# A linear recurrence over eight heads: levels merged, decays in PSUM, head norms on four columns, heads finished inside, output projection begun early

## What is computed

```
f = lb + (1 - lb) * sigmoid(f_pre);  k = 1 - f;  q = silu(q_pre);  v = i_in
b = cumsum(log f) within a chunk of tokens
o_inter = (q * exp(b)) @ state
a[t, s] = sum_d q[t,d] k[s,d] exp(b[t,d] - b[s,d])      for s <= t
o_intra = a @ v
state = exp(b_last) * state + (k * exp(b_last - b))^T @ v
o = o * rsqrt(mean(o*o over the 128 value channels) + eps)
o = o * out_norm * silu(g_pre);  h = h + o @ w_out
```

## Time and profile before

| | |
|---|---|
| median of 3 runs | 3115.41 us (3114.5 to 3117.74) |
| the profiled execution | 3111.95 us, its span 3110.0 us |
| PE busy | 3021.6 us, 97% of the span |
| DVE busy | 2407.8 us, 77% |
| ACT busy | 1193.4 us, 38% |
| POOL busy | 1310.9 us, 42% |
| hg_i's last matmul begins | 1661.6 us |
| the levels run | 1677 to 1810 us |
| hg_out runs | 1822 to 1879 us |

### The profile page before, as it was taken

One profiled execution on the slowest core, in us unless ns is written; L12 is line 12 of the kernel. 1 busy time (PEld: TensorE's weight loads), 2 busy tenths in 40 slices (PEclk: granted clock), 3 DMA queues, 4 the chain that ended last, 5 costly groups with the idle time before them and its releaser, 6 DMA issues.

```text
span 3110.0 us, 44566 instructions
## 1 busy us (share of the span) xinstructions
PE 3021.6 (97%) x16468; PEld 2672.1 (86%) x16468; DVE 2407.8 (77%) x4496; ACT 1193.4 (38%) x1842; POOL 1310.9 (42%) x749
## 2 busy tenths in 40 slices
PE   7999999999999999999998979999999999999998
PEld 5657899999998888887787967899999998888887
DVE  5345899988877888888235876899888978888887
ACT  4433333444433333333333433333444433333333
POOL 3313465444434444443344423465444444444442
PEclk9999999999999999999998989999999999999999
DMA  3202367999999999998221002367999999999996
GB/s 136 73 21 96 99 201 253 341 375 356 374 365 376 372 355 351 356 348 293 88 95 48 1 28 95 102 201 265 336 379 357 373 368 389 361 349 362 351 357 254
DMA packets 345719, 800.86 MB, mean 258 GB/s; under 512 B 27936, under 2 KB 191776, under 8 KB 345248
## 3 DMA queue, kind: packets, MB, share of 16 engines
q1 hardware_dynamic: 271776, 529.55, 48.9%
q0 software_dynamic: 73728, 268.47, 22.7%
HBM read 695.15 MB, written 102.76 MB: 257 GB/s over the span
## 4 chain that ended last, share of the span: by engine, by line
PE 92%; DVE 3%; DMA 2%; ACT 1%; issue 1%; POOL 0%; SPq 0%; ACTq 0%; DVEq 0%
PE PS L1361 27%; PE PS L1363 27%; PE PS L1362 27%; PE PS L1529 3%; PE PS L1626 2%; PE PS L1601 2%; DMA arena<-acts_dram 1%; DVE arena L1327 1%; PE PS L1506 1%; PE PS L1484 1%; DMA acts_dram<-arena 1%; PE PS L1467 1%; PE PS L1466 0%; POOL w_lo L509 0%; DMA w_raw<-in_mla_t 0%
## 5 line engine op out<-in xcount | busy, mean ns | idle before, releaser
L1361 PE MATMUL PS<-x_hi,w_hi 128*128 128x384 f32 (+1 forms) x2616 | 924.9, 354 | 14.7 <-issue 7.5
L586 ACT ACTIVATE w_hi<-w_raw 128x1024 fp32r<-128x1024 f32 x609 | 643.0, 1057 | 699.5 <-PE PS L1363 685.4
L1363 PE MATMUL PS<-x_hi,w_lo 128*128 128x384 f32 (+1 forms) x2616 | 908.3, 347 | 0.0
L1362 PE MATMUL PS<-x_lo,w_hi 128*128 128x384 f32 (+1 forms) x2616 | 907.0, 347 | 0.0
L520 POOL DMA_INDIRECT arena<-in_v_t,arena x256 | 445.1, 1738 | 599.5 <-DVE resid L1173 551.0
L1361 PE MATMUL PS<-w_hi,x_hi 128*128 128x512 f32 x1744 | 682.1, 391 | 12.8 <-POOL w_lo L509 8.6
L1362 PE MATMUL PS<-w_lo,x_hi 128*128 128x512 f32 x1744 | 680.2, 390 | 0.0
L1363 PE MATMUL PS<-w_hi,x_lo 128*128 128x512 f32 x1744 | 679.9, 390 | 0.0
L509 POOL TENSOR_TENSOR w_lo<-w_raw,w_hi 128x1024 fp32r<-128x1024 f32 x169 | 417.7, 2476 | 616.1 <-ACT w_hi L586 616.1
L1150 DVE TENSOR_TENSOR w_lo<-w_raw,w_hi 128x1024 fp32r<-128x1024 f32 x440 | 537.2, 1221 | 107.2 <-ACT w_hi L586 106.9
L520 POOL DMA_INDIRECT arena<-in_u_rows,arena x256 | 380.5, 1486 | 487.7 <-DVE arena L1157 434.5
(11 more groups left out here) (178 smaller groups left out, 2483.7 us busy)
## 6 DMA issues: line engine op xcount, KB each, us to landing
w_raw<-in_u_t SPq DMA_DIRECT2D x256, 512.0 KB, 6.9
w_raw<-in_v_t SPq DMA_DIRECT2D x256, 512.0 KB, 6.7
acts_dram<-arena SPq DMA_DIRECT2D x256, 192.0 KB, 7.4
gates_dram<-arena SPq DMA_DIRECT2D x24, 2048.0 KB, 15.9
arena<-gates_dram SPq DMA_DIRECT2D x64, 768.0 KB, 7.4
arena<-acts_dram SPq DMA_DIRECT2D x256, 192.0 KB, 7.1
w_raw<-in_hg_t SPq DMA_DIRECT2D x40, 512.0 KB, 3.2
w_raw<-in_pq_t SPq DMA_DIRECT2D x32, 512.0 KB, 3.2
```

Source lines behind the costliest of these rows:

```text
L586: act.activation(w_hi[:, slot, :], w_raw[:, slot, :], ACT.Copy).then_inc(hi_ready, 1)
L1361: pe.matmul(ps, wh, xh, start=start, stop=False)
L1362: pe.matmul(ps, wh, xl, start=False, stop=False)
L1363: return pe.matmul(ps, wl, xh, start=False, stop=stop)
```

## The change

It does these things.

1. **Merged levels.** k and q now lie 4096 elements apart with k first, so one access pattern (`keys_and_queries`) names the first halves of k and the second halves of q, and a level is scaled by one DVE instruction of 512 columns. ACT writes the exponentials into PSUM banks 2 and 3 (`scaling`), no longer back into `diff`. So POOL may refill `diff` when ACT is done with it, and `a` has banks 0 and 1 alone.
2. **One matrix a for a head.** `mask_level` writes the diagonal level by a product with its mask and each further level with `copy_predicated` into the places of the same 128x512 matrix. The values are multiplied once for each head (4 matmuls), behind level 7.
3. **Head norms on four columns.** ACT squares; TensorE takes each chunk's squares as the stationary operand and one column of ones as the moving one, which leaves 128x4 sums with tokens on partitions. Mean, root and reciprocal are of 128x4 for a head, the root in three batches (heads 0-3, 4-6, 7). The reciprocal roots come back across partitions by `diagonal` (ACT, four 128x128 products of the identity with a column) and `spread` (TensorE, ones by diagonal).
4. **Heads 0 to 3 are finished (gated, hi, lo) inside heads 6 and 7's levels**, and the first half of their output projection (banks 0 to 3, "project") stands between the last heads' spreads. `hg_out`'s other half rows follow.
5. **hg_i ends token by token** (`APART` = 2 weight tiles at the end instead of 1), its copies out stand among the first levels on ACT, and the four weight tiles of hg_out that POOL and ACT prepared between hg_i and the levels are now prepared in heads 1 and 2.
6. **In all three norms between stages** ACT's last two `next_high` calls stand behind the squares and roots. Before, one of them did (in the norm ahead of the recurrence none).

```diff
+SPREAD_AT = {(5, 6): 0, (6, 3): 1, (6, 6): 2, (7, 3): 3}
+ROOTS = [(0, 4), (4, 7), (7, 8)]
...
-        if n >= 2:
-            yield ("values", *divmod(n - 2, 8))
-            if (n - 2) % 8 == 7:
-                yield "ho", (n - 2) // 8, 0
+            if (h, p) in SPREAD_AT:
+                yield "spread", SPREAD_AT[h, p], 0
+        if n >= 2 and (n - 2) % 8 == 7:
+            yield "values", (n - 2) // 8, 0
+            yield "ho", (n - 2) // 8, 0
...
+    yield "spread", 4, 0
+    yield "project", 0, 0
     yield "hss", HEADS - 1, 0
+    yield "spread", 5, 0
+    yield "spread", 6, 0
+    yield "project", 2, 0
+    yield "spread", 7, 0
...
+        def keys_and_queries(h, m):
+            both = arena[:, h * SEQ:h * SEQ + SEQ]
+            return bass.AP(both.tensor, both.offset,
+                           [list(both.ap[0]), [2 * m, SEQ // (2 * m)], [HEADS * SEQ + m, 2], [1, m]])
...
 # POOL
-                    if (n - 2) % 8 == 0:
-                        pool.wait_ge(sem("k_decayed"), (n - 2) // 8 + 1)
-                    else:
-                        pool.wait_ge(sem("level_x"), (n - 2) // 8 * LEVELS + (n - 2) % 8)
+                    pool.wait_ge(sem("level_exp"), n - 1)
...
-            lows(BASE["hg_q"], BASE["hg_out"] + RING - 1)
+            lows(BASE["hg_q"], BASE["hg_i"] + 8)
             pool.wait_ge(sem("cumulated"), HEADS)
-            for n in range(2):
+            for n in range(8 * HEADS):
                 take_diff(n)
-            lows(BASE["hg_out"] + RING - 1, BASE["hg_out"] + RING)
-            for n in range(2, 8 * HEADS):
-                take_diff(n)
+                if n in range(11, 11 + 2 * RING, 2):
+                    lows(BASE["hg_out"] + (n - 11) // 2, BASE["hg_out"] + (n - 11) // 2 + 1)
...
 # ACT, norm between stages, and the stage ahead of it
-                elif last_tile is not None:
-                    next_high(last_tile)
+                else:
+                    for n in range(last_tile - APART + 1, last_tile + 1):
+                        next_high(n)
-            for n in range(7):
+            for n in range(8 - APART):
                 next_high(BASE["mla_out"] + n)
...
+            def level_exp(n):
+                h, k = divmod(n, 8)
+                act.wait_ge(sem("level_diff"), n + 1)
+                scaling_used(act, n - 2)
+                ...
+                act.activation(halves(scaling(n))[:, :, 0], halves(d)[:, :, 0], ACT.Exp, scale=-1.0)
+                act.activation(halves(scaling(n))[:, :, 1], halves(d)[:, :, 1], ACT.Exp)\
+                   .then_inc(sem("level_exp"), 1)
+            def head_out(h):
+                ready(act, ("ho", h))
+                act.activation(gk[:, h, :], PSb(("ho", h)), ACT.Square).then_inc(sem("head_sq"), 1)
+                free(act.activation(gq[:, h, :], PSb(("ho", h)), ACT.Copy), ("ho", h))
...
+                    if (h, k) == (5, 2):
+                        roots(0)
+                    if (h, k) in ((5, 4), (6, 1), (6, 4), (7, 1)):
+                        diagonal({(5, 4): 0, (6, 1): 1, (6, 4): 2, (7, 1): 3}[h, k], 0)
+                    if (h, k) in ((6, 1), (6, 6), (7, 1), (7, 6)):
+                        gated_high({(6, 1): 0, (6, 6): 1, (7, 1): 2, (7, 6): 3}[h, k])
...
 # DVE
-                for half, src in enumerate((gk, gq)):
-                    ins = dve.tensor_tensor(halves(xx[:, x % 2, :])[:, :, half],
-                                            halves(src[:, h, :])[:, :, half], halves(d)[:, :, half], ALU.mult)
-                ins.then_inc(sem("level_x"), 1)
+                dve.tensor_tensor(halves(xx[:, x % 2, :]), keys_and_queries(h, P >> k), halves(d), ALU.mult)\
+                   .then_inc(sem("level_x"), 1)
...
+                free(dve.copy_predicated(kept, where, given), ("a", h, p))
...
+                if (h, k) in ((6, 0), (6, 5), (7, 0), (7, 5)):
+                    gated({(6, 0): 0, (6, 5): 1, (7, 0): 2, (7, 5): 3}[h, k])
+                if (h, k) in ((6, 2), (6, 7), (7, 2), (7, 7)):
+                    gated_low({(6, 2): 0, (6, 7): 1, (7, 2): 2, (7, 7): 3}[h, k])
...
 # PE
-            token_major("hg_i", 8, 0, lambda kc: None)
-            was_freed(pe, ("hg_i", 7))
+            token_major("hg_i", 8, 0, lambda kc: None, APART)
...
-                    end(pe.matmul(PSb(("hss", h)), ones, gk[:, h, :], start=True, stop=True), ("hss", h))
+                    for c in range(TT):
+                        mm = pe.matmul(PSb(("hss", h))[:, c:c + 1], gk[:, h, c * P:(c + 1) * P], ones[:, 0:1],
+                                       start=True, stop=True)
+                    end(mm, ("hss", h))
```

More of the change, by code:

```diff
@@ L123, in __init__ @@
         self.signals = 0
-        self.count = {"act": 0, "dve": 0, "exp": 0, "state": 0, "kd": 0, "sum": 0}
+        self.count = {"act": 0, "dve": 0, "exp": 0, "state": 0, "kd": 0, "sum": 0, "spread": 0}
         self.turn, self.last = {}, {}
@@ L170, in norm, with eight @@
             b.add(("xT", k, c), "dve")
-    def eight(name, last_tile, frees):
+    def eight(name, last_tile, frees, banks=tuple(range(8))):
         for n in range(8):
-            b.add((name, n), frees, last_tile if n == 7 else None)
+            b.add((name, n), frees, last_tile if n == 7 else None, banks)
     norm(0)
@@ L216, in plan @@
         b.add(("hg_g", n), "act", BASE["hg_g"] + n)
-    eight("hg_i", BASE["hg_i"] + 7, "act")
+    eight("hg_i", BASE["hg_i"] + 7, "act", (2, 3, 0, 1, 4, 5, 6, 7))
     for what, h, p in recurrence():
         if what == "a":
-            b.add(("a", h, p), "dve", None, (0, 1, 2, 3))
-        elif what != "values":
-            b.add((what, h), *{"kd": ("kd", None, (4,)), "st": ("state", None, (5,)),
+            b.add(("a", h, p), "dve", None, (0, 1))
+        elif what not in ("values", "project"):
+            b.add((what, h), *{"spread": ("spread", None, (4,)), "kd": ("kd", None, (4,)), "st": ("state", None, (5,)),
                                "ho": ("act", None, (6, 7)), "hss": ("sum", None, (5,))}[what])
-    eight("hg_out", BASE["hg_out"] + 7, "dve")
+    eight("hg_out", BASE["hg_out"] + 7, "dve", (0, 1, 2, 3, 6, 7, 5, 4))
     peer(1)
@@ L796, in _, with decay @@
                                     PSb(("hg_i", n)), ACT.Copy), ("hg_i", n))
-            for n in range(4, 8):
-                next_high(BASE["hg_i"] + n)
-            def head_out(h):
-                ready(act, ("ho", h))
-                free(act.activation(gq[:, h, :], PSb(("ho", h)), ACT.Copy), ("ho", h))
-            for h in range(HEADS):
+            def decay(h):
                 act.wait_ge(sem("cumulated"), h + 1)
@@ L821, in _ @@
+            for n in range(2):
+                values_out(n)
+            was_freed(act, ("hg_i", 1))
+            decay(0)
+            for n in range(2):
+                level_exp(n)
+            for n in range(2, 8):
+                values_out(n)
+            for h in range(HEADS):
+                if h >= 1:
+                    decay(h)
+                for k in range(8):
+                    if 8 * h + k >= 2:
+                        level_exp(8 * h + k)
                     if k == 2:
```

205 lines of the change are left out of this document (130 added, 75 removed).

## The result

| | before | after |
|---|---|---|
| median, runs of one comparison | 3114.95 us (4 runs) | 3083.31 us (4 runs, 3074.53 to 3085.09) |
| ratio to before, 95% interval | | 0.989 (0.987 to 0.991) |
| profiled execution, its span | 3111.95, 3110.0 us | 3083.25, 3081.2 us |
| forecast | | 3047 us, range 3033 to 3072 |

A forecast was written before the change was run, and what follows sets the result against it. In the levels TensorE's own instructions were taken as the bound, DVE next. Gains of 25.2 (levels), 13.6, 18.0 and 11.1 sum to 67.9 us: 3111.95 to 3044.0, plus 3 gives 3047 us, range 3033 to 3072 for 8 in 10.

The forecast's parts named there:

- Term 1, how they interlock: Levels, per head: TensorE and DVE taking turns add waits of 0.8 and 0.9 us, so 12.2 us instead of 16.8.
- TensorE loses its clock in the levels: Levels: short waits halve TensorE's clock, so a head takes 23.3 us and the whole 3126 us; chance 0.04.
- The turns: Levels, per head: DVE, with 10.2 to 10.9 us of work, waits 0.8 us for TensorE and 0.9 us for ACT.
- The predicated copy: Levels, masks on DVE: the copy costs like 512 columns, 0.60, not 0.34 us; whole time 3065 us; chance 0.14.
- ACT into PSUM: Levels: exponentials written to PSUM cost half more, making ACT the bound, some 1.5 us a head, 3059 us; chance 0.10.
- contention of the scaling: Levels: DVE's merged scaling still meets POOL, 1.2 to 1.35 us instead of 0.60; whole time 3086 us; chance 0.06.
- Lo parts in heads 1 and 2: Heads 1 and 2: four lo parts on POOL, each beside two differences, add 5 us to the levels.
- finishing in heads 5 to 7: Levels: head 5's table loads and root add 2.1 us; four heads finished inside heads 6 and 7 add 6.
- Front: From hg_i's end to the first level: 1.4 us instead of 15.0, a gain of 13.6 us.
- Norms: Three norms between stages: squares follow as tokens come, gaining 4.1 + 4.4 + 2.6 = 11.1 us.
- Tail: From last mask to hg_out's end: 51.0 us or so instead of 69.1, a gain of 18.0 us.

## Why the prediction was half right

- **The step that failed is "Term 1, how they interlock", with the clock taken as 1.00.** It priced a head at 12.2 us; it takes 18.5. Two errors add up, and the gain of 25.2 us in the levels became a loss of 7.5.
- **The clock.** With one extra matmul the same turns at 1.00 give 14.9 us (TensorE idle for 1.48 of it) where after has 18.5 to 18.7 at 0.68: some 3.6 us a head, or more, since the 14.9 has the extras in it. The rival "TensorE loses its clock in the levels" had the mechanism and got a chance of 0.04; its price, 23.3 us a head, was too high, since the clock comes back in each head and doesn't stay down. I set it aside because the share of TensorE's time would be 89% and 63% had still had 0.95. A share over 18 us did not tell: within the head, TensorE is busy for 79, 77 and 60% of the three windows of 2 us from 1715 on, and in the last of them the clock fell. That was to be had from the prediction's own model, in which TensorE waits in every level. The Trainium skill (TensorE: Matmul & The Clock Gate, A second HAM failure mode) describes this for bf16 matmuls of 512 columns, a clock that goes up and down with short idles between groups that cycle through PSUM banks. Here the trace agrees: 0.50 to 1.00 and back, with averages of 0.67 to 0.71 over heads 1 to 5.
- **The turns.** 14.9 less 12.2 is 2.7 us a head. DVE's work was near (10.2 to 10.9 forecast, 11.3 found, with some 0.6 of it the copy on levels 6 and 7). Its waits were not: 1.7 us forecast, and in the head with one extra matmul 3.6, of which 2.12 is for ACT. I had put 0.9 for ACT's square and copy and left out that ACT first waits 1.50 us for the finished head. Of the 2.7 us the extra matmuls may be some 0.5 (an estimate: two pairs, with pitches of 0.22 and 0.28, stand ahead of the state's matmuls for which ACT waits); no run has the changed kernel's own list at full clock. Two smaller readings were off: the 1.06 taken for a level group is the row of a value group, and a level group lasts 1.00; and no row stands behind the 0.3 us of signals. In after DVE's scaling begins 0.10 us behind the level that it waits for (1709.72 + 1.81, then 1711.63).
- **The predicated copy** was a rival as a whole (0.60 on every level). It is 0.43 on five levels, as taken, and 0.72 on two, some 0.6 us a head more than forecast. The columns are the same on all seven; what differs is the length of the runs.
- **ACT into PSUM, contention of the scaling:** both rivals fell. An exponential takes 0.39, before 0.41; a scaling 0.68 to 0.84.
- **Lo parts in heads 1 and 2, 5 us; finishing in heads 5 to 7, 8 us.** With the clock held by two extra matmuls heads 1 and 2 take 15.46 and 15.37, as the others: the lo parts hide. Heads 5 and 6 take 1.7 and 2.3 us more.
- **Front:** 13.6 forecast, 13.8 found. **Norms:** 11.1, 12.9 in the trace and 10.9 by their own run. **Tail:** 18.0, 15.3, and what is missing is about what four groups lost at half clock (2.8 us).
- **Outside the change,** 4.5 us were lost before the first norm in the profiled run, in code that is the same. The clock of the attention differs: 0.74 in 132 to 160 us here, 1.00 before. Over the profiled executions of the other kernels, the five with 1.00 in this window end the attention's output at 249.5 to 253.2 us, the ten with 0.71 to 0.82 at 255.5 to 257.6. It is likely why the runs of one kernel lie up to 11 us apart (3074.53 to 3085.09). After and the kernel with two extra matmuls have the same list there, with 0.74 in one and 1.00 in the other, so the edits of the levels don't decide it.

The levels missed by 140.8 - 108.1 = 32.7 us. The kernel with two extra matmuls, whose clock is 1.00 throughout, has its first level at 1655.28 and ends its last mask, DVE's

```profile
1777.64 1.55 DVE L1337 COPY_PREDICATED arena<-mask_bits,PS 128x256 f32<-128x256 uint16 x2
```

at 1779.1: 123.8 us. So holding the clock gives back 17.0 us of the miss, net of what the extra matmuls cost. The other 15.7 are the turns, with what is left of the extra matmuls' own time in them, which no run separates. What stays open is why one extra matmul a level holds the clock in heads 3 and 4, with waits of 0.19 to 0.78 us left, and the runs don't tell whether the length of a wait or their sequence decides.

## What to carry to other kernels

Where an engine is to be relieved of work, ask what its clock does with the gaps: here a third of TensorE's instructions were taken from a loop of turns, and each of those left took up to twice as long. If the waits can't be closed, a few matmuls of no use in them can pay (0.989 to 0.983), and better is to close the loop first and fill what is left (0.980). Before a piece of POOL's work is put beside DVE's, look which of DVE's instructions there read two inputs from SBUF: one such product cost 1.7 us and then the clock (2.43 us instead of 0.74). And ask of every pass on a helper engine not only what it costs but what it waits for while others stand behind it.

## What the hardware showed that was not expected

- With TensorE busy for 13.44 of 14.92 us (90%) and waits of up to 0.78 us the clock stayed at 1.00 over two heads; in head 3 of after it fell behind waits of 0.43, 0.47 and 0.79 us ahead of three levels in a row, and in the kernel with ACT's passes later, one extra and the third buffer behind a single one of 2.95 us.
- `copy_predicated` of 128x256 from PSUM: 0.41 to 0.44 us with runs of 4 elements or more (40 rows of after), 0.71 to 0.73 with runs of 2 and 1 (16 rows). The merged scaling took 0.68 to 0.72, and 0.80 to 0.84 with runs of one.
- Two-input DVE instructions from SBUF: a pair of 128x256 took 3.67 us beside a difference and a lo part of POOL, 0.75 alone; a product of 128x512 took 2.43 beside a lo part, 0.74 alone.
- Two table loads of 1.28 us stand in head 5 of after, each right behind the instruction ahead of it: the first of those ends at 1747.77, and the load begins at 1747.79.
